# Layer 0's context experts dense instead of gathered, on one core of a Trainium2

## What is computed

```
q = (h @ w_q).reshape(T, 8 heads, 2, 128);  s = q . sub_keys        # 128 scores per half
s1, i1 = top_k(s[.., 0], 16);  s2, i2 = top_k(s[.., 1], 16)
top_s, pos = top_k(s1[:, None] + s2[None, :], 16)                    # 16 of 256 pairs
idx = i1[pos // 16] * 128 + i2[pos % 16];  gate = softmax(top_s)     # 8 x 16 experts of 16384
out = sum over the 128 experts e of  gate * gelu(h . u[e]) * v[e]
```

## Time and profile before

| | |
|---|---|
| times of three runs | 2715.65, 2709.63, 2709.32 us |
| span of the profiled execution | 2712.5 us |
| instructions | 23250 |
| busy | PE 1912.4, DVE 1686.8, POOL 1678.7, ACT 387.6 us |
| HBM read | 958.53 MB, of which 805.40 MB by POOL's queue (gathers) |
| mean granted TensorE clock | 0.824 |

### The profile page before, as it was taken

One profiled execution on the slowest core, in us unless ns is written; L12 is line 12 of the kernel. 1 busy time (PEld: TensorE's weight loads), 2 busy tenths in 40 slices (PEclk: granted clock), 3 DMA queues, 4 the chain that ended last, 5 costly groups with the idle time before them and its releaser, 6 DMA issues.

```text
span 2712.5 us, 23250 instructions
## 1 busy us (share of the span) xinstructions
PE 1912.4 (71%) x7346; PEld 811.1 (30%) x7346; DVE 1686.8 (62%) x4224; ACT 387.6 (14%) x800; POOL 1678.7 (62%) x1542
## 2 busy tenths in 40 slices
PE   6999658787787866656666765668646986666556
PEld 2455532222353322222112211224542442221111
DVE  2333887667797776776444756553497966666641
ACT  1122112012131111000101111111112210101000
POOL 0000357777777777777555775773157776777775
PEclk9999879998878978887766787889767987777779
DMA  6473779999999999999999999996599999999999
GB/s 235 138 266 109 271 280 401 405 406 405 405 329 385 402 406 404 386 408 408 402 402 403 392 385 385 342 388 238 175 325 379 397 371 401 406 406 390 391 389 360
DMA packets 317705, 961.18 MB, mean 354 GB/s; under 512 B 30208, under 2 KB 65168, under 8 KB 317200
## 3 DMA queue, kind: packets, MB, share of 16 engines
q0 software_dynamic: 221184, 805.40, 76.3%
q1 hardware_dynamic: 92240, 146.34, 15.2%
q10 hardware_dynamic: 4160, 7.95, 0.8%
HBM read 958.53 MB, written 1.05 MB: 354 GB/s over the span
## 4 chain that ended last, share of the span: by engine, by line
POOL 27%; PE 25%; DMA 24%; DVE 12%; issue 11%; ACT 1%; SPq 0%; POOLq 0%; DVEq 0%; ACTq 0%
DMA v_rows<-in_peer_v,idx_turned 16%; POOL u_rows L465 14%; POOL v_rows L465 12%; PE ps L897 8%; DVE u_rows L1757 5%; PE ps L612 4%; DMA u_rows<-in_peer_u,idx 4%; PE ps L824 3%; PE ps L863 1%; PE ps L512 1%; DMA u_rows<-in_peer_v,idx_turned 1%; DMA wring<-in_mod_w 1%; PE ps L523 1%; DMA h<-in_peer_v,idx_turned 1%; PE ps L650 1%
## 5 line engine op out<-in xcount | busy, mean ns | idle before, releaser
L465 POOL DMA_INDIRECT u_rows<-in_peer_u,idx x768 | 853.5, 1111 | 677.4 <-DVE idx L1686 376.2
L1757 DVE CUSTOM_DVE_ANT_0 u_rows<-u_rows,h 128x1024 f32<-128x1024 f32 x768 | 930.6, 1224 | 538.6 <-DMA u_rows<-in_peer_u,idx 529.1
L897 PE MATMUL ps<-v_rows,spread_w 128*32 128x512 f32 x2636 | 849.8, 773 | 518.9 <-DMA v_rows<-in_peer_v,idx_turned 472.4
L465 POOL DMA_INDIRECT v_rows<-in_peer_v,idx_turned x659 | 708.8, 1075 | 307.4 <-issue 166.8
L897 PEld LDWEIGHTS ps<-v_rows,spread_w 128*32 128x32 f32 x2636 | 165.7, 127 | 1043.8 <-issue 1024.3
L612 PE MATMUL ps<-wring,arena 128*128 128x512 f32 x528 | 250.9, 624 | 13.3 <-DVE arena L1268 8.1
L863 PE MATMUL ps<-arena,wring 128*128 128x256 f32 (+1 forms) x1024 | 202.0, 357 | 4.9 <-ACT h L1128 2.7
L863 PEld LDWEIGHTS ps<-arena,wring 128*128 128x128 f32 x1024 | 173.4, 214 | 59.6 <-issue 37.9
L612 PEld LDWEIGHTS ps<-wring,arena 128*128 128x128 f32 x528 | 100.9, 199 | 165.5 <-issue 151.7
L512 PE MATMUL ps<-table,arena 128*128 128x128 f32 x432 | 80.8, 316 | 75.3 <-ACT arena L948 31.7
L523 PE MATMUL ps<-wring,silu_c 128*32 128x512 f32 x384 | 107.4, 742 | 9.1 <-DMA wring<-in_mod_w 9.1
(11 more groups left out here) (219 smaller groups left out, 1891.9 us busy)
## 6 DMA issues: line engine op xcount, KB each, us to landing
wring<-in_mod_w SPq DMA_DIRECT2D x96, 512.0 KB, 8.1
wring<-in_peer_w_q SPq DMA_DIRECT2D x64, 512.0 KB, 10.4
wring<-in_ab_w_in SPq DMA_DIRECT2D x56, 512.0 KB, 6.1
wring<-in_swa_w_in SPq DMA_DIRECT2D x28, 512.0 KB, 10.0
u_rows<-in_peer_u,idx POOLq DMA_INDIRECT x768, 9.5
v_rows<-in_peer_v,idx_turned POOLq DMA_INDIRECT x659, 10.1
wring<-in_ab_w_out SPq DMA_DIRECT2D x16, 512.0 KB, 4.8
wring<-in_swa_w_out SPq DMA_DIRECT2D x16, 512.0 KB, 8.6
```

The lines of the kernel that those rows point to most:

```text
L465: nc.gpsimd.indirect_dma_start(out=rows, out_offset=None, in_=table, in_offset=bass.IndirectOffsetOnAxis(ap=index, axis=0)).then_inc(lande ...
L897: mm = nc.tensor.matmul(PS[32 * q:32 * q + 32, 6 + e, :], spread_w[:, s // PAIR % 2, 32 * c:32 * c + 32], v_buffer(v_place(x)[0])[:, e * 5 ...
L1757: nc.vector.tensor_tensor_reduce(UB[:, slot % NU, :], UB[:, slot % NU, :], H2[:, g // 8 % 3, :], 1.0, 0.0, ALU.mult, ALU.add, av_[:, 0, g ...
```

## The change

Tiles 0 and 1 (the 256 context tokens of layer 0) are no longer gathered. Their routing is done for all heads on DVE (`dense_routes`), and the gates are put into a matrix in DRAM, `GATES`, of 16384 experts x 256 tokens: POOL writes it full of zeros in 16 DMAs during the head, and then issues 2 x 128 indirect DMAs that each add 128 gates (one per token), waiting after each 16 for their landing. PE, ACT and DVE then compute all 16384 experts for the 256 tokens in 128 blocks (`dense`): SP streams 128 rows of u, of v, and the gates; PE turns the u block (8 transposes), multiplies it with `h` (8 matmuls with 256 columns); ACT takes the gelu; DVE multiplies with the gates; PE multiplies with the v block (4 matmuls with 512 columns) into four PSUM banks over all 128 blocks. The dense steps stand in the window of the latent tiles, one block per slot, slots 56 to 190.

prep(0) and the latent mixer move ahead of the first window, which now has two tiles (256 slots). The gather windows' numbers of tiles shrink by two everywhere, the held scores move from tile 1 to tile 2, and the norm output of the context tiles goes into two of the u buffers (`h2_row`).

```diff
+ND = 2
+PT_ = ND * P
+EXPERTS = 16384
+NBLK = EXPERTS // P
+RING = 4
+NGE = 8
+VLAG = 4
...
-        WINDOWS = [(0, 4), (4, 6)]
+        WINDOWS = [(0, 2), (2, 4)]
...
-        BESIDE = {0: table_of((c_prep(0)[READY[0]:], 1, 34), (c1[:-12], 34, 14 * TOPK + 8),
-                              ([1.0] * 12, 2 * S1 - 10, 2 * S1 + 86), ([1.8] + [3.4] * 24 + [1.0], 2 * S1 + 86, 3 * S1 + 18),
...
+        BESIDE = {0: table_of((c_prep(1)[READY[1]:], 1, 34), ([1.8] + [3.4] * 24 + [1.0], 34, 56), (c_dense, 56, 190),
+                              (c_norm(2) + c_proj(2), 190, 212), (c2, 212, 2 * S1 + LAG - 8)),
...
+            def dense_loads():
+
+                for i in range(NBLK):
+                    if i % 4 == 0:
+                        j = i // 4
+                        if j == 0:
+                            sp.wait_ge(g_put[0], 16 * S1)
+                            sp.wait_ge(g_put[1], 16 * S1)
+                            sp.wait_ge(tp_done, 32)
+                        if j >= 2:
+                            sp.wait_ge(d_w, 4 * (j - 1))
+                        rows = GATES[4 * j * P * PT_:4 * (j + 1) * P * PT_, :]
+                        sp.dma_start(GB[:, j % 2, :, :], rows.rearrange("(i p t) o -> p i (t o)", i=4, p=P)).then_inc(gb_in[j % 2], 16)
+                    if i == 0:
+                        sp.wait_ge(rt_pv, 2 * HEADS0)
+                    if i >= RING:
+                        sp.wait_ge(d_tr, 2 * (i - RING + 1))
+                    sp.dma_start(UR[:, i % RING, :], a["peer_u0"][i * P:(i + 1) * P, :]).then_inc(ur_in[i % RING], 16)
+                    if i >= 2:
+                        expert_values(i - 2)
...
+            def expert_values(i):
...
+                if i >= RING:
+                    sp.wait_ge(d_v, i - RING + 1)
+                sp.dma_start(VR[:, i % RING, :], a["peer_v0"][i * P:(i + 1) * P, :]).then_inc(vr_in[i % RING], 16)
...
             for n, (_, kind, l, b, split, half, part, _) in enumerate(blocks):
+                if n == dense_at:
+                    dense_loads()
...
-            pool.wait_ge(rt_m, HEADS0)
+            pool.wait_ge(sw_zero, 1)
+            for c in range(16):
+                pool.wait_ge(*((pr_mm, c + 1) if c < 12 else (op_mm, c - 11)))
+                rows = GATES[c * EXPERTS * PT_ // 16:(c + 1) * EXPERTS * PT_ // 16, :]
+                nc.gpsimd.dma_start(rows.rearrange("(p n) o -> p (n o)", p=P),
+                                    spread_w[:, :, :].rearrange("p b n -> p (b n)")[:, 0:2048]).then_inc(g_zero, 16)
+            pool.wait_ge(g_zero, 256)
+            for e in range(ND):
+                pool.wait_ge(d_gate, e + 1)
+                for s in range(S1):
+                    if s % TOPK == 0 and s:
+                        pool.wait_ge(g_put[e], 16 * s)
+                    nc.gpsimd.indirect_dma_start(
+                        out=GATES, out_offset=bass.IndirectOffsetOnAxis(ap=S_IDX[:, e, s:s + 1], axis=0),
+                        in_=S_G[:, e, s:s + 1], in_offset=None, compute_op=ALU.add).then_inc(g_put[e], 16)
...
+            def dense():            # PE
...
+                for i in range(NBLK + VLAG):
+                    if i + 1 < NBLK:
+                        turned_block(i + 1, 0)
+                    if i < NBLK:
+                        pe.wait_ge(d_ut, 2 * i + 2)
+                        if i >= 2:
+                            pe.wait_ge(d_gelu, i - 1)
+                        for k in range(KC):
+                            mm = nc.tensor.matmul(PS[:, 1, i % 2 * PT_:(i % 2 + 1) * PT_], UT[i % 2][:, k, :], HDT[:, k, :],
+                                                  start=k == 0, stop=k == KC - 1)
+                        mm.then_inc(d_u, 1)
+                    if i + 1 < NBLK:
+                        turned_block(i + 1, 1)
+                    m = i - VLAG
+                    if m >= 0:
+                        pe.wait_ge(d_w, m + 1)
+                        pe.wait_ge(vr_in[m % RING], 16 * (m // RING + 1))
+                        for e in range(ND):
+                            for half in range(2):
+                                mm = nc.tensor.matmul(PS[:, 4 - 2 * e + half, :], GE[:, m % NGE, e * P:(e + 1) * P],
+                                                      VR[:, m % RING, half * 512:(half + 1) * 512], start=m == 0, stop=m == NBLK - 1,
+                                                      skip_group_check=True)
+                        mm.then_inc(d_v, 1)
+                    yield
...
-            rest = ready_and_route(0)
-            gathers(0, 4, chain(rest, norm1(1), proj(1), attn(1), ret(1), outp(1), prep(1),
-                                row_g2(1), ada(1, range(12)), norm1(2), proj(2), norm1(3), proj(3), attn(EARLY), rows2()))
+            for _ in chain(prep(0), beside(chain(norm1(1), proj(1)), dense_routes()), attn(1), ret(1), outp(1)):
+                pass
+            rest = ready_and_route(1)
+            gathers(0, 2, chain(rest, row_g2(1), ada(1, range(12)), dense(), norm1(2), proj(2), norm1(3), proj(3), attn(EARLY), rows2()))
```

More of the change, by code:

```diff
@@ L916, in _ @@
             rest = ready(2, prep(2))
-            gathers(4, 6, chain(rest, row_g2(2), proj(5), attn(4), outp(3), prep(3)))
+            gathers(2, 4, chain(rest, row_g2(2), proj(5), attn(4), outp(3), prep(3)))
         @block.scalar
@@ L1195, in _ @@
                 pass
-            rest = ready(0, prep(0))
-            gathers(0, 4, chain(rest, norm1(1), proj(1), attn(1), ret(1), outp(1), prep(1),
-                                row_g2(1), ada(1, range(12)), norm1(2), proj(2), norm1(3), proj(3), attn(EARLY), rows2()))
+            for _ in chain(prep(0), beside(chain(norm1(1), proj(1)), dense_exps()), attn(1), ret(1), outp(1)):
+                pass
+            rest = ready(1, prep(1))
+            gathers(0, 2, chain(rest, row_g2(1), ada(1, range(12)), dense(), norm1(2), proj(2), norm1(3), proj(3), attn(EARLY), rows2()))
             for _ in chain(norm1(4), proj(4), attn_late(), outp(2)):
@@ L1622, in prep @@
                         todo = [(PS[:, 2 + m % 2, e * P:(e + 1) * P], TOPV[:, (t0 + e) % 3, m, :], TOPI[:, (t0 + e) % 3, m, :],
-                                 rest_s[:, e, :]) for e in range(1 if p == 0 and m in HELD else nt)]
+                                 rest_s[:, e, :]) for e in range(1 if p == 1 and m in HELD else nt)]
                         for s, tv, ti, sp_ in todo:
@@ L1736, in ready_and_route @@
                     next(steps)
-                route(8 * T_OF[p])
+                route(8 * (T_OF[p] - ND))
                 return steps
```

281 lines of the change are left out of this document (231 added, 50 removed).

## The result

The changed kernel takes 3366.34 us (median of 4 runs, 3354.49 to 3369.23), beside 2712.64 us for the kernel before in the same set. The ratio is 1.2396, 95% interval [1.2370, 1.2423]: 24% slower. The profiled execution is the fastest of the four, with a span of 3352.7 us; its stages add up to this span.

The account below looks back on a forecast made before the run. TensorE's chain bounds the head, DMA the gather windows; after the change PE bounds the dense part. 2712.5 + 450 (start) + 85 (window) = 3248, say 3250 us, 20% slower; forecast 3170 to 3350 (0.68), range 3080 to 3450.

Parts of the forecast that it names:

- The start: Ahead of the first window: the first gather leaves at 735 us instead of 285, +450, once POOL's scatters are issued.
- Price of a scatter: On POOL's queue before the first gather: 1.24 us per issue, taken from a gather, 256 x 1.24 = 317 us.
- The 14 waits: On POOL's queue: 14 waits until 16 scatters have landed, 2.5 us each, 35 us.
- rival 2: Before the first gather: scatters run one at a time, window start 921, total 3436 us; chance 0.13 with worse cases.
- Zero writes: In the head: 16 writes of 1.05 MB, hidden at a DMA share of 0.54; 42 us if not.
- First gates: Before the first scatter: the gates of tile 0 are ready at 383 us.
- The compute chain: Ahead of the first gather: prep(0), then the latent mixer up to its first route, done at 622 us.
- The window: First gather window: 87 + 120 + 1197 + 266 = 1670 us against 1585 before, +85.
- Dense part: Inside the first window: 134 slots bound by PE, 8.05 us per block plus 0.92 per gather slot, 1197 us at clock 0.98.
- The u load: In the dense slots: queued on SP, about one slot, 9.8 us, to land; just holds, else the slot is about 9.5.
- Rival 4: Whole kernel: the change does not cut traffic, so bytes read would not fall by about 117 MB; no chance given.
- Rival 3: Dense block bound by DMA, 5.6 us per slot; with the start at 622 the kernel is faster, 2688 us; chance 0.04.

Follow-up runs that it names:

- the first experiment: The changed kernel with 16 scatters per tile instead of 128, without the waits between them, 7 of 8 gates left out: 3197.07 us, ratio 1.1282.

## Why the prediction was right, and where its sizes were off

The forecast was 3250 us, measured are 3366, inside the range of 3080 to 3450 but 16 us above the 3170 to 3350 that had the chance of 0.68. The mechanism was right in the main: PE becomes the bound of the dense part, POOL's scatters hold the start, the second window stays. The sizes were off, and in part they cancel: against the forecast of 3248 the start came 188 us later, the window 75 us and the end 8 us shorter, which makes the span of 3352.7. That the total is only 3 to 4% off owes something to luck.

1. **The start: forecast +450, measured +637.6.** This is the largest miss. It has three terms.
   - *Price of a scatter: 1.24 us assumed, from a gather's issue.* Measured 1.578 + 0.30 = 1.88, so 256 x 0.64 = 164 us more. The addition causes it: without it the same instruction is 0.96. The 14 waits cost 516 - 481 = 35 us, as forecast, though a landing takes 3.0 us and not 2.5. The issue, not the landing, is the price; rival 2's 921 came close to the measured 923 only by number. Scatters overlap: they leave every 1.85 us though each lands after 3.0.
   - *Zero writes: "hidden".* They weren't. Late ones bring the first gather 13.7 us forward in the pair of profiles compared above. The DMA share of 0.54 was an average over the head; in 140:215 of the kernel before it is 0.72, and beside the writes PE waits there for weights.
   - *First gates: forecast 383, measured 407.* 12 of the 24 are the later head (prep(0) starts at 276.3 instead of 263.9), the rest is my estimate of prep(0)'s steps and of the routing.
2. **The compute chain: forecast 622, measured 684.** It was hidden by the scatters, so it cost nothing here, but with the scatters gone it is the next bound (696 in the first experiment). Stage by stage the 62 us are a sum of misses with both signs. The head was 12 us late. prep(0)'s steps and the norm took 87.0 us (276.3 to 363.3) instead of 70, the projection 103, as forecast. Dense routing was charged 37 us on top; it can only show in the 87.0 (78.9 in the kernel with the mixer ahead alone). Attention and retention took 146.6 us (466.2 to 612.8) instead of the 77.7 of the context tiles (136.1 to 213.9), 69 us more; from there on both take 71.5. The stretch of the context tiles, in the kernel before:

```profile
136.00:214.00 78.00, 76.78 (x449) 43.66 (x450) 25.01 (x74) 16.36 (x44) 0.00 (x0) 0.98 0.73 252
```

PE was at a clock of 0.98 there, and 44.7 of its 76.8 us were modulation and the retention's projection (lines 523, 539 and 730 of the kernel before), which the latent stretch doesn't have. The latent attention and retention alone therefore take PE four times as long (128.90 against 32): twice the records in most of their products, wider scores, and a clock of 0.51. The pace of one mixer was taken for another's. At full clock 128.90 us would be about half; no run brought that clock about.
3. **The window: forecast 1670, measured 1594.**
   - First 32 slots 87, measured 86. The slots up to the dense part 120, measured 126 for 25 slots and 8 more to the first u product. The last part 266, measured 248.3.
   - Dense part 1197, measured 1125.6. A block of 7.76 us instead of 8.05 (four transposes take 0.44, not 0.53, and four v products 3.43, not 3.54) is 37 us; the clock is 1.00, not 0.98, 23 us; filling and leaving took 9 us, not 20.
   - The u load held: PE never waited for it in 1200:2200. With light blocks it did, at 6.6 us per slot; here a slot takes 8.5.
4. **Traffic.** Read are 841.09 MB, before 958.53, 117 less, as the count of gathers, blocks and gates gives. Rival 4 falls.
5. **Rival 3** (DMA-bound, 2688) was rightly dismissed for float32. Its number, 2688, is near the 2696 us of the kernel with light blocks and few scatters, but by luck: there the first gather leaves at 676.8 instead of 622, and the window takes 1179 us instead of 1223. Its dense part of 750 us compares with 706 in bf16. By the Trainium skill ("TensorE: Matmul & The Clock Gate", Back-to-back issue gap) 512 columns take 216 ns. The trace has eight records in 3.43 us (1503.25 to 1506.68), 0.86 us for each of four float32 matmuls, four times that. For float32 the measurement decides. In bf16, one record per matmul, eight products of 256 columns take 0.87 us and four of 512 take 0.96 (1500.05 to 1502.35 in the bf16 kernel), 0.11 and 0.24 us each.

Where the gain of half the gathers went: with products in bf16 the window does shrink, to 1183.5 us (920.8 to 2104.3), 400 less than before. The float32 products take all of it back (1594.2). The start then adds its 638: 356 for the mixer set ahead (641.6 in the kernel with that alone), 55 for what else stands there with few scatters (696.2), and 227 for the rest of the scatters. Of the 55, 20 are the later head of that profile (prep(0) starts at 286.1, against 265.7), and some 31 the first steps of prep(1), its norm and first query projections, which run ahead of the first route (653.25 to 684.35 in the changed kernel).

## What to carry to other kernels

Trading gathers for dense products can pay only if the dense block costs PE less than its bytes cost DMA: price a block in records of its own type before counting bytes. Work that a kernel does beside its gathers costs little there and its full length once it stands ahead of them (356 us ahead, 56 back in the window); in bf16, where the window shrinks by 400 us, that alone takes back most of the gain. Count the instructions on the queue that issues the gathers, each at the price of its own form: 256 issues of 1.9 us were the longest step of the start.

## What the runs showed of the hardware

- An indirect scatter with an addition costs POOL 1.55 us of issue (1.58 in the mean), a plain one 0.96, a gather 0.94 at its quickest and 1.05 in the mean. 0.30 us stand between two.
- Beside plain scatters in batches of 16 DVE, ACT and TensorE stalled in steps of up to 26 us and more (TensorE busy 75.8 of 300 us in 500:800); beside batches of 4, on another chip, they didn't (164.7 us).
- The granted clock was at its lower level (0.50 to 0.51) in the latent attention, with PE busy 88% in the changed kernel and 97% with the extra matmuls, and at 1.00 in the dense part with PE busy 100%. It fell behind a wait of 5.36 us.
- Mixed gathers and block loads reached 404 GB/s on one core.
- Two profiles of the changed kernel differ in the head's clock (140:215: 0.91 and 0.64) by 20 us in the first gather (922.9 and 943.0) and by 27 in the span (3352.7 and 3380.0). The later start of prep(0) (295.6 against 276.3) is 19 us of that. Part of the spread of 15 to 40 us between runs of one kernel may come from there; that wasn't tried.
